# The first PEER head's queries computed with tokens as the stationary operand, and turned afterwards

## The reference

```python
q      = xn @ peer_w_q                      # 8 heads x 256 wide, two halves of 128
s0, s1 = q_half0 @ sub_keys0.T, q_half1 @ sub_keys1.T   # two lists of 128 scores a head
top16 of s0, top16 of s1 -> 16x16 sums -> top16 of the sums   # 16 experts a head
expert = index0 * 128 + index1              # one of 16384
out   += sum over 16 experts of softmax(score) * gelu(u[expert] . xn) * v[expert]
```

## Time and profile before

| | |
|---|---|
| median of 3 runs | 1737.49 us (1736.73 to 1737.63) |
| the profiled execution | 1736.6 us, of which the span of the profile is 1734.8 us |
| TensorE (PE) | 1607.2 us busy, 93% of the span |
| VectorE (DVE) | 1166.5 us, 67% |
| ScalarE (ACT) | 861.0 us, 50% |
| GpSimd (POOL) | 358.3 us, 21% |
| gathers (queue q0) | 268.45 MB of 463.92 MB in all |

### The profile page before, as it was taken

How to read it: one execution, slowest core, us unless ns; L and a number is a source line. 1 busy time by engine, 2 the same in 40 slices (tenths; PEclk the granted TensorE clock), 3 DMA queues, 4 the chain that set the end, 5 groups by cost and what they waited for, 6 DMA issues and landing times.

```text
span 1734.8 us, 21427 instructions
## 1 busy us (share of the span) xinstructions
PE 1607.2 (93%) x8184; PEld 1182.6 (68%) x8184; DVE 1166.5 (67%) x2051; ACT 861.0 (50%) x1566; POOL 358.3 (21%) x381
## 2 busy tenths in 40 slices
PE   9999999999999999999999999899977787777786
PEld 7988998888998899888889998555422232222232
DVE  6657766666765876666675557887767677666654
ACT  5556635443455654444455545555444544444443
POOL 0200000000020000000060102545544444444330
PEclk9999999999999999999999999999999999999999
DMA  8443554555544355455544366999999999999996
GB/s 312 158 145 123 181 206 171 194 179 189 197 146 146 124 194 205 174 191 194 191 150 146 146 218 266 400 422 420 421 422 421 421 421 422 422 422 421 422 421 272
DMA packets 67209, 463.92 MB, mean 267 GB/s; under 512 B 7458, under 2 KB 9634, under 8 KB 11939
## 3 DMA queue, kind: packets, MB, share of 16 engines
q0 software_dynamic: 36864, 268.45, 37.3%
q1 hardware_dynamic: 29952, 193.77, 30.7%
q10 hardware_dynamic: 290, 0.33, 0.1%
HBM read 461.48 MB, written 1.05 MB: 267 GB/s over the span
## 4 chain that ended last, share of the span: by engine, by line
PE 61%; DMA 23%; DVE 6%; issue 4%; ACT 3%; POOL 2%; POOLq 0%; ACTq 0%; DVEq 0%
PE acc L611 13%; PE acc L613 13%; PE acc L612 13%; DMA row_w_hi<-in_peer_uv,arena 7%; DMA arena<-in_peer_uv,arena 6%; DMA row_xa<-in_peer_uv,arena 5%; PE att L636 5%; PE acc L636 3%; PE att L637 3%; DMA row_w_lo<-in_peer_uv,arena 2%; PE acc L1793 2%; PE acc L1796 2%; DMA row_xb<-in_peer_uv,arena 2%; PE acc L637 1%; DVE w_lo L573 1%
## 5 line engine op out<-in xcount | busy, mean ns | idle before, releaser
L573 DVE TENSOR_TENSOR w_lo<-arena,w_hi 128x2048 fp32r<-128x2048 f32 x170 | 388.6, 2295 | 162.0 <-ACT w_hi L566 161.5
L566 ACT CAST w_hi<-arena 128x2048 fp32r<-128x2048 f32 x174 | 331.9, 1909 | 118.8 <-PE acc L613 98.5
L1924 ACT ACTIVATE arena<-arena,small 128x1 f32<-128x1 f32 x256 | 75.4, 294 | 286.5 <-DVE arena L2286 136.6
L2286 DVE SCALAR_TENSOR_TENSOR arena<-arena 128x1024 f32<-128x1024 f32 x122 | 149.0, 1224 | 86.5 <-DMA arena<-in_peer_uv,arena 85.9
L611 PE MATMUL acc<-xa,w_hi 128*128 128x256 f32 x672 | 192.4, 286 | 0.4 <-DVE w_lo L573 0.4
L612 PE MATMUL acc<-xa,w_lo 128*128 128x256 f32 x672 | 190.0, 283 | 0.0
L613 PE MATMUL acc<-xa,w_hi 128*128 128x256 f32 x672 | 190.0, 283 | 0.0
L1793 PE MATMUL acc<-arena,gate_raw 128*128 128x512 f32 x244 | 134.0, 632 | 46.6 <-ACT gate_raw L1934 43.6
L2507 POOL DMA_INDIRECT arena<-in_peer_uv,arena x122 | 136.3, 1117 | 162.9 <-PE acc L1796 132.0
L636 PE MATMUL att<-xa,w_hi 128*128 128x512 f32 x384 | 136.0, 398 | 0.0
L611 PEld LDWEIGHTS acc<-xa,w_hi 128*128 128x128 f32 x672 | 128.6, 191 | 4.6 <-issue 3.6
(11 more groups left out here) (345 smaller groups left out, 3511.9 us busy)
## 6 DMA issues: line engine op xcount, KB each, us to landing
arena<-in_units SPq DMA_DIRECT2D x174, 1024.0 KB, 4.8
arena<-in_units SPq DMA_DIRECT2D x4, 512.0 KB, 6.9
arena<-in_bias SPq DMA_DIRECT2D x1, 2048.0 KB, 9.3
arena<-in_peer_uv,arena POOLq DMA_INDIRECT x122, 39.9
x_res<-in_x SPq DMA_DIRECT2D x2, 512.0 KB, 6.3
arena<-in_norm_mlp_g SPq DMA_DIRECT2D x2, 512.0 KB, 6.7
arena<-in_norm_g SPq DMA_DIRECT2D x2, 512.0 KB, 6.5
arena<-in_final_norm_g SPq DMA_DIRECT2D x2, 512.0 KB, 5.8
```

What stands on the lines that cost most here:

```text
L566: nc.scalar.copy(w_hi[:, s, :], raw[HOME[g]]).then_inc(S["hi_ready"], 1)
L573: nc.vector.tensor_tensor(w_lo[:, s, :], raw[HOME[g]], w_hi[:, s, :].bitcast(F32), ALU.subtract).then_inc(S["lo_ready"], 1)
L2286: nc.vector.scalar_tensor_tensor(row, row, 1.0, hn[:, n // SLOTS, :], ALU.mult, ALU.mult, accum_out=dots[:, n:n + 1]).then_inc(S["rows_use ...
```

## The change

The first head's queries are now computed the other way round: stationary are 128 tokens, moving are the 256 weight columns of the head (8 blocks x 3 passes = 24 matmuls a tile, where there were 48). The result has tokens on partitions. ScalarE copies it to memory (`query_copy`), TensorE turns it with two transposes (`turn_queries`), and ScalarE copies that to its place (`query_turned`). Both lists' scores of tile 0 are made by two matmuls in a row with one signal, and copied out by one instruction of 256 columns (`rank_take(0, [0])`) in place of two of 128. The four blocks of `mix` 3 for tile 1 are spread: one before the transposes, one before the scores, two after the half tile's transposes. VectorE waits once for both lists, and does the low part of tile 1's first half (`tile_dve`) after all of `first_experts` and not in the middle of it. For tile 1, the turning comes behind `other_queries(1)` on TensorE, and its copy behind item 0's diagonal on ScalarE.

```diff
-            def queries_of(t, n_, ks):
+            def queries_of(t, ks):
...
-                    m = passes(QUERY_BANKS[t, n_][:, n_ * SEQ + t * P:n_ * SEQ + (t + 1) * P], h[:, k, n_ * P:(n_ + 1) * P],
-                               lw[:, k, n_ * P:(n_ + 1) * P], xb_hi[:, k, tok], xb_lo[:, k, tok], k == 0, k == 7)
+                    m = passes(QUERY_BANKS[t], xb_hi[:, k, tok], xb_lo[:, k, tok], h[:, k, :], lw[:, k, :], k == 0, k == 7)
...
+            def turn_queries(t):
+
+                pe.wait_ge(S["query_in"], at("query_in", ("by token", t)))
+                for i in range(2):
+                    m = nc.tensor.transpose(att[1][:, i * P:(i + 1) * P], q_tokens[:, t, i * P:(i + 1) * P], ident[:])
+                m.then_inc(S["query_done"], mark("query_done", ("turned", t)))
...
             def first_queries():
...
-                queries_of(0, 0, range(8))
-                queries_of(0, 1, range(4))
-                rank_half(0)
-                queries_of(0, 1, range(4, 8))
+                queries_of(0, range(8))
+                tile_of_mix(1, 3, range(1))
+                turn_queries(0)
+                tile_of_mix(1, 3, range(1, 2))
+                pe.wait_ge(S["query_in"], at("query_in", ("turned", 0)))
+                for i in range(2):
+                    m = nc.tensor.matmul(att[0][:, i * P:(i + 1) * P], queries[:, i, 0:P], keys[:, i, :], start=True, stop=True)
+                m.then_inc(S["rank_done"], mark("rank_done", (0, 0)))
                 half_pe(pe, "n2", 1, 0)
-                rank_half(1)
-                tile_of_mix(1, 3).then_inc(S["unit_done"], mark("unit_done", ("u", at_unit2["mix", 3])))
+                tile_of_mix(1, 3, range(2, 4)).then_inc(S["unit_done"], mark("unit_done", ("u", at_unit2["mix", 3])))
                 emptied2(pe, "mix", 2)
-                queries_of(1, 0, range(4))
-                queries_of(1, 1, range(4))
+                queries_of(1, range(4))
                 half_pe(pe, "n2", 1, 1)
                 for _ in range(4):
                     nc.tensor.matmul(acc[1][:, 0:P], ident[:], ident[:], start=True, stop=True)
-                queries_of(1, 0, range(4, 8))
-                queries_of(1, 1, range(4, 8))
+                queries_of(1, range(4, 8))
...
             other_queries(1)
+            turn_queries(1)
             row_times_coefficient(0)
...
-            first_take(0)
-            first_rank(0)
-            first_take(1)
+            query_copy(0)
+            query_turned(0)
+            rank_take(0, [0])
             tile_act(act, xb_hi, "n2", 1, [0])
-            first_rank(1)
...
             peer_square(1)
+            query_copy(1)
             weight_exp(0)
...
-            take("pq", 0)
             for n in range(ITEMS):
                 diagonal(n)
                 if n == 0:
+                    query_turned(1)
                     split_hi(act, at_unit2["pq", 2])
...
             first_experts()
+            tile_dve(dve, xb_hi, xb_lo, "n2", 1, [0])
             second_tile()
```

57 lines of the change are left out of this document (26 added, 31 removed).

## The result

| | before | changed kernel |
|---|---|---|
| median, first comparison (20 runs each) | 1737.07 us (1736.39 to 1737.91) | 1739.34 us (1737.5 to 1741.6) |
| median, second comparison (27 runs of before, 11 of the changed) | 1737.34 us | 1738.51 us (1737.68 to 1740.5) |
| profiled execution, span | 1736.6, 1734.8 us | 1739.48, 1737.7 us |

The ratio is 1.0014 (95% interval 1.0008 to 1.0020) in the first comparison and 1.0009 (1.0000 to 1.0018) in the second: 2.3 and 1.2 us slower, and both together speak for a small loss and not for chance, though the second interval touches 1. That is inside the 0.2% that the prediction called "within" and inside its range, but of the other sign than the forecast of -0.26 us.

What follows compares the result with a forecast made beforehand. Gathers run at 421 GB/s from 1140 us, so their start and empty DMA time before fix the end. The 1.39 us gain shrinks to 0.26 at item 1's diagonal: 1737.49 - 0.26 = 1737.2 us, range 1735.4 to 1739.6.

Steps and rivals of the forecast that it cites:

- within: Whole kernel: time differs from the kernel before by no more than 0.2%, 3.5 us; chance 0.87.
- the first rival: TensorE before tile 1's query matmuls: clock falls, item 1's diagonal 1.2 us later, 1738.7 us; chance 0.35.
- Tile 0, gain 1.39 us: Tile 0 up to the first gather: fewer query matmuls and shorter serial copies issue item 0 1.39 us earlier, at 1072.45.
- The wait of 3.1 us: TensorE before tile 1's first query matmuls: waits 3.1 us for the low part moved behind L2213, where before nothing.
- The clock: TensorE's new wait before tile 1: a fall to 1.2 GHz is about as likely as not.
- stays up: TensorE after the new wait: clock stays full, so the forecast of 1737.2 us holds; chance 0.45.
- The price of the fall: Tile 1's 12 query matmuls take 0.24 each, 1.44 us late; item 1's diagonal at 1087.4, 1.2 us later.
- The prediction's own sign of being wrong: Item 1's diagonal over 1 us earlier or later, or another length of the stage after 1140 us.
- Item 0's diagonal: ScalarE: item 0's diagonal earlier by about 1.1 us, from removed copies and item 0's earlier landing.
- ScalarE as what is late next: ScalarE's strict list: `query_turned(1)` delays `pq` 2 to 1083.69, item 1's diagonal to 1085.97; 1.39 us gain becomes 0.26.
- The holes: Gather traffic before 1140 us: first hole about 1.4 us shorter, second about 1.1 us longer; afterwards the same 421 GB/s.
- The lower end of the range: Whole kernel: fastest time in the range, 1735.4 us, from the head start's 1736.1 and the runs' 0.9 us spread.

Runs made afterwards that it cites:

- the low part came earlier: Changed kernel with ScalarE's turned-queries copy behind `pq` 2's high part and VectorE's low part ahead of the cast in `first_experts`: 1736.07 us, again 1736.20 us.
- the first experiment: Changed kernel with 12 identity matmuls in TensorE's new wait before tile 1's first query matmuls: 1738.66 us against 1737.53, ratio 1.0005.
- both mended: Changed kernel with 12 identity matmuls in TensorE's wait and ScalarE's turned-queries copy behind `pq` 2's high part: 1736.08 us, ratio 0.9993; again 1736.18, 0.9991.

## Why the prediction was wrong

The mechanism that decided was in the text, as the first rival, and the forecast was given to the other one.

- **Tile 0, gain 1.39 us: right.** 24 matmuls at 0.12, two copies of 0.37 (0.38 taken), the scaled one 0.47 (0.46), L2214 at 1071.20 (forecast 1071.31), item 0 at 1072.34 (1072.45), 1.50 us gained.
- **The wait of 3.1 us: right**, 3.35 measured.
- **The clock: the step that failed.** "A fall is about as likely as not", and the likelier branch was given to "stays up" with 0.45 against 0.35 on the strength of one row of sparse work that kept its clock after 2.84 us. In all four profiles with a wait of 3.35 us here the clock fell (0.53, 0.76, 0.76, 0.76), and with both new waits filled the change as written took the time of before (0.9999). The Trainium skill, "TensorE: Matmul & The Clock Gate", in "Loop structure matters more than you think", says that long waits between bursts of matmuls bring the clock down, and the trace agrees for this wait; the rival that went with it had 1738.7 us, and the medians are 1739.34 and 1738.51. I weighed it against one row where the engine came from other work, and let the row decide. What that section of the Trainium skill says would not have told the fall's length, nor that a wait of 2.33 us left the clock up when the low part came earlier.
- **The price of the fall: one figure for something that varies.** The rival had 12 x 0.12 = 1.44 us and item 1 1.2 us later than before. In the first profile that was too small, since the four transposes and four filling matmuls behind the 12 also run at half speed, and the first of the last 12: last query matmuls 1.62 us later than forecast, 1.97 later than with the clock held up, the copy on ScalarE 2.2 us, item 1 at +1.54. In the second it was too large: last query matmuls at 1076.55, 0.90 us later than forecast, the copy 1.2 us, item 1 at +0.57. That the rival's 1738.7 us lies between the two medians is partly luck. The prediction's own sign of being wrong, item 1 over 1 us late, holds in the first profile and not in the second.
- **Item 0's diagonal: forecast 1.1 us earlier**, and 1.56 us earlier with the clock held up (1080.09); with the fall it was 0.39 us later in the first profile and 0.33 us earlier in the second.
- **ScalarE as what is late next: right.** Forecast: `query_turned(1)` at 1083.4, `pq` 2 at 1083.69, item 1 at 1085.97. With the clock held up: 1083.01, 1083.28, 1085.56.
- **A wait that I did not see.** When item 1's diagonal is held by ScalarE while item 0's is early, TensorE stands still 1.98 us between them (0.64 before). The clock may fall there, and did in the first experiment. The prediction put no term there.
- **The holes: right in kind.** The first filled by 1.6 us (1.4 forecast). What was given back is 3.9 us and not 1.1, and most of it lies beside the hole that I had named: before it, where the six places had run out, and behind it up to 1115.5 us. How the loss is shared among the holes is not firm, as the second profile of the kernel before shows. From 1140 us the rate did not change, as forecast.
- **The lower end of the range.** By its own working it is 1736.1 - 0.9 = 1735.2 us and not 1735.4; nothing hangs on it here.

What stays open: in the first profile of the changed kernel item 39 is issued 1.77 us late and the end comes 2.9 us late, in the second 1.14 and 1.1. The two profiles of the kernel before differ by 0.5 us over the same part, so 0.5 of the 1.2 us that the first one adds after item 39 can be chance of the execution; whether the rest is too was not settled. Where between item 12 and item 17 a further fall of the clock comes in, and what it costs, was not tested. The medians of the two comparisons, 2.3 and 1.2 us, leave the same span open. Nor is it known why the fall lasts longer in one execution than in another.

## What to carry to other kernels

An instruction of 0.7 us that is moved out of another engine's way is not paid by its own length but by the wait it leaves on TensorE: where a change gives TensorE a new wait behind full work, work the forecast out with the matmuls behind it at 1.2 GHz, and keep the other level as the rival until a trace shows it. Where an engine's strict list gets a new wait, ask how much work the awaited instruction stands behind on its own engine; moving it half a unit forward there, or the waiting one behind the next two instructions here, gave 1.2 to 1.6 us at item 1. With both mended the same change was 0.07 to 0.09% faster than the kernel before by its ratios (0.9993 and 0.9991; the intervals, 0.9982 to 1.0002, reach 1), and not 0.09 to 0.14% slower; that it is faster than the unmended change is clear of the spread of the runs.

## What the runs showed of the hardware that I had not expected

- The clock's answer to one and the same wait differs between executions: 3.35 us gave 0.53 once and 0.76 three times over the same 7 us; 1.98 us before item 1 left it up in both profiles of the changed kernel and with the first filling was followed by a fall to 0.81 over 9 us; 2.12 us let it fall in the kernel before with the low part moved, 2.33 us did not with the low part earlier. The fall need not come in the wait: it began 1.1 us before the matmuls started in the first profile of the changed kernel and 0.7 us after it in the second. Length alone doesn't decide.
- Twelve float32 products of the identity, in a wait of 3.35 us, held the clock at 1.00 from 1070.5 to 1077.5 us in each of the four profiles that had them, though three of these have a fall later (0.90 from 1098.5 to 1115.5 us), and left 0.6 us of idle time in front of the next real matmul; none made that matmul later (1071.77 to 1072.02 against 1071.91 to 1072.11 without them).
- A scaled copy of 256 columns from PSUM takes 0.47 us and a plain one 0.37 us; turning the operands round took the price of a query matmul from 0.110 us with 128 columns moving to 0.12 us with 256, so half the matmuls at 1.09 times the price.
